# Softmax weights on 64 rows, a gate joined with its output product, and head products in one instruction

## The reference, cut to what matters

```python
wts = jax.nn.softmax(jnp.stack(lses), axis=0)
o = jnp.sum(wts[..., None] * jnp.stack(outs).astype(jnp.float32), axis=0)
return (o * jax.nn.silu(z)) @ w_out
```

```python
g = jax.nn.gelu(y)
y = g * jax.nn.sigmoid(g @ w_glu + b_glu)
return (y * jax.nn.silu(z)) @ w_out
```

## Time and profile before

| | |
|---|---|
| time, median of 3 runs | 4006.62 us (4005.82 to 4010.16) |
| the profiled execution's own time | 4003.77 us |
| its span | 4002.0 us |
| PE busy | 3653.1 us (91%) |
| DVE, ACT, POOL busy | 42%, 22%, 48% of the span |
| mean granted clock of TensorE | 0.943 |
| combining stage | 607.2 to 683.4 us of the span |
| gate stage, split stage | 960.7 to 1009.8 us, 1010.1 to 1015.6 us |
| out product of the state space layer | 1015.9 to 1070.5 us |
| heads of the recurrence | 1981.8 to 2181.7 us |

### The profile page before, as it was taken

How to read it: one execution, slowest core, us unless ns; L and a number is a source line. 1 busy time by engine, 2 the same in 40 slices (tenths; PEclk the granted TensorE clock), 3 DMA queues, 4 the chain that set the end, 5 groups by cost and what they waited for, 6 DMA issues and landing times. The chain is left out here.

```text
span 4002.0 us, 47523 instructions
## 1 busy us (share of the span) xinstructions
PE 3653.1 (91%) x18444; PEld 2985.3 (75%) x18444; DVE 1691.3 (42%) x2710; ACT 896.4 (22%) x2349; POOL 1905.6 (48%) x749
## 2 busy tenths in 40 slices
PE   8999996798888899999966999998999998889999
PEld 6787873677776788878756888876888877678887
DVE  5523236887366422144375411337411236642213
ACT  2333332222134211111132100126100023421111
POOL 5444430523532365555643555651566553236554
PEclk9999995887999899999988999998999999889999
DMA  4236861243221222222201222230222222122221
GB/s 139 85 128 92 111 98 54 68 120 87 91 74 64 79 95 96 102 86 91 82 1 37 86 102 96 93 107 27 107 95 94 95 96 74 64 79 95 96 102 76
DMA packets 96530, 346.75 MB, mean 87 GB/s; under 512 B 27270, under 2 KB 45958, under 8 KB 61528
## 3 DMA queue, kind: packets, MB, share of 16 engines
q1 hardware_dynamic: 83984, 318.45, 26.6%
q10 hardware_dynamic: 12360, 25.70, 1.9%
HBM read 321.04 MB, written 18.87 MB: 85 GB/s over the span
## 5 line engine op out<-in xcount | busy, mean ns | idle before, releaser
L294 POOL CAST wh<-raw 128x2048 fp32r<-128x2048 f32 x269 | 512.8, 1906 | 1670.0 <-PE bank L336 1273.3
L296 POOL TENSOR_TENSOR wl<-raw,wh 128x2048 fp32r<-128x2048 f32 x269 | 1245.9, 4632 | 21.5
L334 PE MATMUL bank<-XTh,wh 128*128 128x512 f32 (+1 forms) x2448 | 951.1, 389 | 45.0 <-DVE XTl L1167 15.1
L336 PE MATMUL bank<-XTl,wh 128*128 128x512 f32 (+1 forms) x2448 | 935.3, 382 | 0.0
L335 PE MATMUL bank<-XTh,wl 128*128 128x512 f32 (+1 forms) x2448 | 934.7, 382 | 0.0
L334 PEld LDWEIGHTS bank<-XTh,wh 128*128 128x128 f32 x2448 | 467.5, 191 | 155.5 <-issue 41.8
L336 PEld LDWEIGHTS bank<-XTl,wh 128*128 128x128 f32 x2448 | 465.8, 190 | 89.8
L335 PEld LDWEIGHTS bank<-XTh,wl 128*128 128x128 f32 x2448 | 468.0, 191 | 84.6
L334 PE MATMUL bank<-wh,XTh 128*128 128x512 f32 (+2 forms) x1056 | 392.8, 372 | 37.9 <-DVE XTl L1167 12.6
L335 PE MATMUL bank<-wh,HTl 128*128 128x512 f32 x1024 | 403.4, 394 | 0.0
L334 PE MATMUL bank<-wh,HTh 128*128 128x512 f32 x1024 | 401.7, 392 | 0.0
(11 more groups left out here) (355 smaller groups left out, 4035.6 us busy)
## 6 DMA issues: line engine op xcount, KB each, us to landing
raw<-in_weights SPq DMA_DIRECT2D x270, 1024.0 KB, 4.8
B<-bias_d ACTq DMA_DIRECT2D x8, 1024.0 KB, 5.7
...
bias_d<-O SPq DMA_DIRECT2D x16, 256.0 KB, 21.3
MO<-HS SPq DMA_DIRECT2D x64, 64.0 KB, 2.8
...
```

The costliest lines, as they stand in the source:

```text
L294: pool.tensor_copy(wh[s][:, :], raw[r][:, :]).then_inc(w_high.h, 1)
L296: pool.tensor_tensor(wl[s][:, :], raw[r][:, :], wh[s][:, :].bitcast(F32), ALU.subtract).then_inc(w_split.h, 1)
L334: nc.tensor.matmul(psum, sh, mh, start=first, stop=False)
L336: return nc.tensor.matmul(psum, sh, ml, start=False, stop=last)
```

## The change

It has three parts.

1. `combine_groups` holds the weights on 64 rows by 128 columns for each group (a head and a token's remainder or block make a row) where it had 16 rows by 512. Two transposes and four small matmuls replace the 12 transposes; `quarters` is a new small input. A product with a 0/1 pattern (`spread`) and three products (`share`) make 64 rows by 512 columns for the selector matmuls, and `sel` now has 64 rows (256 KB). The three matmuls of a p go to three banks of their own, `tile2_free` comes behind the third product, all sigmoids are taken ahead, `acc` is doubled, and the low part of p-1 is subtracted behind the products of p.
2. `hgrn_heads`: POOL no longer subtracts for steps 0 and 2; ACT takes their exponentials straight from `LF` with a column as bias, in 4 pieces of 128 and 8 of 64 columns. For steps 2 to 8 DVE multiplies both halves in one instruction, whose second operand steps between `KIN` and `QF` (now one tensor `KQ`).
3. `SsmGate` replaces `ssm_gate` and `split_features` and runs inside `out_phase`'s block. The gated values are split tile by tile into buffers of their own (`XGh`, `XGl`), gate tiles use banks 4 to 7, and the out product waits for split tiles instead of block ends. `N` shares the memory of `U`.

```diff
+def quarters():
+
+    p = np.arange(P)[:, None]
+    return np.concatenate([p // 4 == np.arange(32), p % 4 == np.arange(4)], axis=1).astype(np.float32)
...
+            xs = gate.split if gate else (XTh, XTl)
...
-                N = sb("N", [P, TT, D], F32, c)
+                if gate is None:
+                    N = sb("N", [P, TT, D], F32, c)
+                else:
+                    N = gate.U[:, :, :].rearrange("p a n -> p (a n)").rearrange("p (t d) -> p t d", t=TT)
...
+                        if gate is not None:
+                            gate.pool(pool)
                         split(0, 3)
...
+                            if gate is not None:
+                                gate.wait_split(pe, 4 * kh + 4)
                             r = t_tile(bank(half, tt), (c0 + kh) % SPLIT, [(kk, 4 * kh + kk) for kk in range(4)],
-                                       (XTh, XTl), natural(tt), kh == 0, kh == 1)
+                                       xs, natural(tt), kh == 0, kh == 1)
...
+                        if gate is not None:
+                            gate.pe(pe)
                         for kh in range(2):
                             for tt in range(TT):
                                 out_tile(0, tt, kh)
...
-                        sp.dma_start(sel[:, :, :], t["head_select"]).then_inc(loaded.h, 16)
+                        sp.dma_start(quarter[:, :], t["quarters"]).then_inc(loaded.h, 16)
+                        sp.dma_start(sel[:, :, :], t["head_select"]).then_inc(selectors.h, 16)
...
                         for p in range(8):
-                            if p >= 2:
-                                act.wait_ge(tile2_free.h, tile2_free.base + p - 1)
-                            a.activation(sg[:, p % 2, :], YF[:, p, :], ACT.Sigmoid).then_inc(a_b.h, 1)
+                            a.activation(sg[:, p, :], YF[:, p, :], ACT.Sigmoid).then_inc(a_b.h, 1)
+                        for p in range(8):
...
-                        for s in range(12):
-                            r = nc.tensor.transpose(PS[s // 4][0:HEADS, P * (s % 4):P * (s % 4) + P], SM[:, :, s], ident[:, :])
+                        for g in (1, 2):
+                            nc.tensor.transpose(PS[0][0:4 * HEADS, P * g:P * g + P], logs[:, g, :, :], ident[:, :])
+                        for tt in range(TT):
+                            r = nc.tensor.matmul(PS[0][0:4 * HEADS, 32 * tt:32 * tt + 32], picked[:, tt, :, :], quarter[:, 0:32], start=True, stop=True)
                         r.then_inc(p_b.h, 1)
-                        pe.wait_ge(b_p.h, b_p.base + 2)
-                        pe.wait_ge(loaded.h, loaded.base + 16)
+                        pe.wait_ge(selectors.h, selectors.base + 16)
                         for p in range(8):
                             if p >= 2:
                                 pe.wait_ge(tile2_free.h, tile2_free.base + p - 1)
                             for g in range(3):
-                                r = nc.tensor.matmul(PS[4 * (p % 2) + g][:, :], sel[:, p, :], LR[:, g, :], start=True, stop=True)
-                            r.then_inc(p_b.h, 1)
+                                if p == 0:
+                                    pe.wait_ge(b_p.h, b_p.base + 2 + g)
+                                nc.tensor.matmul(PS[1 + 3 * (p % 2) + g][:, :], sel[:, p, :], share[:, g, :, :], start=True, stop=True).then_inc(p_b.h, 1)
...
+                        by_group = [x[:, :, :].rearrange("p h (g r) -> p g h r", r=4) for x in (SM, MX)]
+                        link(v.tensor_tensor(logs[:, :, :, :], by_group[0], by_group[1], ALU.subtract))
+                        dve.wait_ge(loaded.h, loaded.base + 16)
+                        v.tensor_tensor(picked[:, :, :, :], logs[:, 0, :, :].rearrange("p h t -> p t h").unsqueeze(3).to_broadcast([P, TT, HEADS, 4]),
+                                        mod4.unsqueeze(1).unsqueeze(1).to_broadcast([P, TT, HEADS, 4]), ALU.mult).then_inc(b_p.h, 1)
...
+                        link(v.tensor_copy(LR[:, :, :].rearrange("q g l -> q (g l)"), PS[0][0:4 * HEADS, 0:3 * P]))
...
+                        link(v.tensor_tensor(spread[:, :, :], M[:, :].unsqueeze(2).to_broadcast([4 * HEADS, P, 4]),
+                                             mod4[0:4 * HEADS].unsqueeze(1).to_broadcast([4 * HEADS, P, 4]), ALU.mult))
+                        for g in range(3):
+                            v.tensor_tensor(share[:, g, :, :], spread[:, :, :], LR[:, g, :].unsqueeze(2).to_broadcast([4 * HEADS, P, 4]), ALU.mult).then_inc(b_p.h, 1)
+
+                        def gate(p):
+                            dve.wait_ge(a_b.h, a_b.base + 3 + p)
+                            v.tensor_tensor(YF[:, p, :], YF[:, p, :], sg[:, p, :], ALU.mult).then_inc(gated.h, 1)
+
+                        def weigh(p, g, to):
+                            dve.wait_ge(p_b.h, p_b.base + 2 + 3 * p + g)
+                            return v.tensor_tensor(to, O3[:, p, g, :], PS[1 + 3 * (p % 2) + g][:, :], ALU.mult)
+
+                        def low(p):
+                            dve.wait_ge(a_p.h, a_p.base + p + 1)
+                            link(v.tensor_tensor(XTl[:, p, :], acc[:, p % 2, :], XTh[:, p, :].bitcast(F32), ALU.subtract))
+                        gate(0)
+
...
+                            x = acc[:, p % 2, :]
+                            link(weigh(p, 0, x))
+                            link(weigh(p, 1, part[:, 0, :]))
+                            link(v.tensor_tensor(x, x, part[:, 0, :], ALU.add))
+                            link(weigh(p, 2, part[:, 1, :]))
+                            dve.sem_inc(tile2_free.h, 1)
+                            link(v.tensor_tensor(x, x, part[:, 1, :], ALU.add))
+                            dve.wait_ge(gated.h, gated.base + p + 1)
+                            v.tensor_tensor(x, x, YF[:, p, :], ALU.mult).then_inc(b_a.h, 1)
+                            if p < 7:
+                                gate(p + 1)
+
+                            if p:
+                                low(p - 1)
+                        low(7)
                         link.done()
...
-                    QF = sb("QF", [P, KT, S], F32, c2)
-                    KIN = sb("KIN", [P, KT, S], F32, c2)
+                    KQ = sb("KQ", [P, 2, KT, S], F32, c2)
+                    KIN, QF = KQ[:, 0], KQ[:, 1]
...
-                                for n in [0] + list(range(2, 9)):
+                                for n in range(3, 9):
...
+
+                        order = InOrder(act, act_order)
+                        order(a.activation(middles[:, :, :], LF[:, :, P // 2 - 1:S:P], ACT.Copy, scale=-1.0))
+                        order.done()
...
-                                    if n in (1, 9):
+                                    if n in (0, 1, 2, 9):
                                         at(act, WF, i, SL, SL * b + n - SLOTS + 1)
                                     else:
-                                        at(act, PD, i, 8, 8 * b + (1 if n == 0 else n))
+                                        at(act, PD, i, 6, 6 * b + n - 2)
                                     x = w(2 * i + b, n)
                                     if n == 1:
                                         r = a.activation(x, of(KIN, i, b), ACT.Copy)
                                     elif n == 9:
                                         r = a.activation(x, of(LF, i, b), ACT.Exp)
                                     elif n == 0:
-                                        r = a.activation(x, x, ACT.Exp)
+                                        g = of(LF, i, b)
+                                        for cc in range(TT):
+                                            cs = slice(P * cc, P * cc + P)
+                                            r = a.activation(x[:, cs], g[:, cs], ACT.Exp, scale=-1.0, bias=g[:, P * cc + P - 1:P * cc + P])
+                                    elif n == 2:
+                                        g, half = of(LF, i, b), P // 2
+                                        for cc in range(TT):
+                                            lo, mid = P * cc, P * cc + half
+                                            a.activation(x[:, lo:mid], g[:, lo:mid], ACT.Exp, scale=-1.0, bias=g[:, mid - 1:mid])
+                                            r = a.activation(x[:, mid:lo + P], g[:, mid:lo + P], ACT.Exp, bias=middles[:, 2 * i + b, cc:cc + 1])
...
-                                        x3, half = blocks(x, n - 2), P >> (n - 1)
-                                        kin, q = blocks(of(KIN, i, b), n - 2), blocks(of(QF, i, b), n - 2)
-                                        link(v.tensor_tensor(x3[:, :, 0:half], x3[:, :, 0:half], kin[:, :, 0:half], ALU.mult))
-                                        v.tensor_tensor(x3[:, :, half:], x3[:, :, half:], q[:, :, half:], ALU.mult).then_inc(DW.h, 1)
+                                        half, k = P >> (n - 1), KIN[:, 2 * i + b, :]
```

(78 more changed lines are left out.)

144 lines of the change are left out of this document (45 added, 99 removed).

## The result

The changed kernel took 3946.9 us (median of 4 runs, 3941.8 to 3958.4) against 4006.2 for the kernel before: a ratio of 0.9856, 95% interval 0.9831 to 0.9881. It is 59 us faster where 41 were summed, and lies 4 us under the range of the prediction (3951 to 3982). The profiled execution took 3943.4 us with a span of 3941.6, to be set against 4003.8 and 4002.0.

A forecast was written before the change was run, and what follows sets the result against it. The prediction took a chain of stages mostly set by TensorE's matmuls as the bound; gains of 17.7, 11.3 and 12 sum to 41.0 us, from 4003.8 to 3962.8, forecast as 3966 with 2.8 for the median; range 3951 to 3982.

The forecast's parts named there:

- Part 1: Combining stage: shorter front and VectorE steps without waits for ACT's copies gain 17.7 us, bounds 14 to 19.
- Part 3: Gate into out product: TensorE goes on without idling or slow clock, gain 11.3 us, bounds 8 to 12.
- without them 43.6: Last gate tile to last out tile: 43.6 us once the 2.6 us of slow clock are gone.
- Part 2: Recurrence heads: joint product and less contention with GpSimd save 1.5 us a head, gain 12, bounds 2 and 18.
- I take 0.5 off; bounds 0 and 1.2: Heads: fewer GpSimd subtractions and fewer products offered cut VectorE's contention by 0.5 us a head.
- The other term: Heads, steps 3 to 7: one product instead of two saves 0.20 us a level, 1.0 us a head.
- the rival of a rising clock: TensorE's clock rises: 1.3 us in the combining stage, 1.5 to 2.5 us a head; 3946 to 3954; chance 0.09.
- Idle time before the first merge as before: Heads: VectorE's wait ahead of each head's first merge stays, 4.53 us, 33.8 over all 64 merges.
- The other side: Heads: GpSimd catches the joint product at six levels, 0.85 us more 48 times, 41 us; 4007 or more; chance 0.03.
- Step 8's product: Heads: operand jumping at every element makes it 1.0 us against 0.80 before, hidden in idle time before EL.
- the 0.4 of the row: Heads, step 8: a traced product jumping at every element, 1.10 us against 0.69, implies 0.4 more.
- the 0.35 of the rule: Heads: by the skill's rule on runs under two words, step 8 alone pays, some 0.35 us a head.

The follow-up runs named there:

- joint_only: Kernel before with KIN and QF in one tensor and one VectorE product a level, GpSimd's 64 subtractions kept: 3979.0 us against 4006.9, ratio 0.9929.
- tiny_joint: joint_only with GpSimd's 64 subtractions in the heads cut to one element each and their exponentials at scale 0: 3971.4 us, one run.

## Why the prediction was right or wrong

**Part 1** was right: 17.7 us summed, 18.0 measured, and the same 18.0 in all nine traces of kernels that have it. The first share was ready 7.9 us after the subtraction instead of 7.7 (it begins at 7.2), the reciprocal 0.94 where 1.0 was scaled from its columns, and the steps 5.67 us instead of 5.8. The rival's 1.3 us from TensorE's clock did not come: it stayed at 0.50 with 64 rows too.

**Part 3** was right in its mechanism, and a good 1 us too high: 11.3 summed, 54.84 - 44.79 = 10.05 measured. VectorE's order came out as laid down, 1.96 + 5.38 + 0.67 behind the odd tile and 0.68 + 1.10 + 0.69 behind the even one, and TensorE never stood still. The term that failed is "without them 43.6", taken over from the old buffers: it measured 44.79, since the new ones start 32 bytes past a multiple of 64.

**Part 2** is where the prediction failed: gain 12 summed, 22.3 measured (means of five traces without and five with it), in the term of the contention: "I take 0.5 off; bounds 0 and 1.2". The other term, 1.0 us a head for the fixed cost of the second product, measured 0.85 (0.16 a level for 0.20). But of the contention only a third of line 2674's 1.6 us a head was taken off, for the number of subtractions (8 to 6) and of offers. It is the seam that matters: all 64 subtractions can stay, and the products still get shorter by 65.6 - 42.5 = 23.1 us, of which 47.6 - 39.8 = 7.8 are fixed cost and 15.3 contention. Taken by head, joint_only's section is 2.79 us shorter, of which 0.85 are fixed and 1.9 contention (1.4 against the shortest section of the five, 15.21), where the prediction took 0.5 off and bounded it by 1.2. The steps had shown it already: 1.56 was read off one level that nothing disturbed, where the median levels of the stage were 2.30 and 2.36. That the two exponentials on ACT are part of the gain was wrong too: with two products they are worth 5 to 10 us in the stage, beside the joint product they cost 4.5, and why they do stays open.

Beside it the rival of a rising clock came in part: the mean in the heads went from 0.79 to 0.87 and TensorE's part of a head from 7.99 to 7.39 us, 4 of the 25.5 us between the first and the last merge (8 sections of 2.67 are 21.4). The clock stood at 0.50 for 10.2 us of a head before and for 5.3 after. The rival had a chance of 0.09 and was costed at 1.5 to 2.5 us a head; 0.6 came. "Idle time before the first merge as before" was wrong for this reason: 33.8 us over all merges became 28.4.

The other side, GpSimd catching the joint product at every level, is the opposite of what happened: mean 0.816 us, and six catches of 1.40 us in the eight heads, each at the level behind the gated products, where GpSimd gets in while VectorE works from a bank. One more catch lies outside the products: `EL`, a copy of 4 columns, took 0.97 us in the head shown where it took 0.17 (means over the heads 0.69 and 0.49).

**Step 8's product.** It took 0.84 us against 0.69 for levels that nothing held, and lay ahead of a wait of `EL` for ACT, which is 0.84 in the head shown and was 0.46. So the hop cost 0.15 us, hidden, as it was placed; the 0.4 of the row and the 0.35 of the rule were both too much. The rule of the Trainium skill (Vector Engine (DVE) Microarchitecture Reference, 5.2 Measured stream behaviour on trn2) is borne out in kind: in tiny_joint, where no subtraction holds anything up, the levels with runs of two words and more take 0.68 to 0.69 us, and only the level of single words takes 0.84. In size the trace has (0.84 - 0.17)/512 = 1.3 ns a column where the page has 1.73.

**The rest**, 59 against the 50 to 51 that the parts give, is within the interval of the first comparison (48 to 68 us). What its trace shows of it was no step of the prediction but its silent premise, that stages whose code is the same take the same time. They differ by up to 13.2 us between two executions of one kernel. With 3 runs of before as base the prediction had 4006.6 us; 57 runs on four chips gave medians from 3997.4 to 4006.9. Against the mean of the heads over five traces the change is worth 18.0 + 11 + 22.3 = 51 us, and the two later comparisons gave 53 and 55 us. So some 10 us of the miss of 18 are the contention and the clock in the heads; the rest is no more than the difference between executions. With its diff attention as long as in the trace before, the profiled execution would have taken some 3957 us (my estimate, 3943.4 + 13.3).
